# Output products, queries and expert search of a tile placed among the attention units of the next tile

## The chip, the cores and the metric
The kernel runs on one core of one Trainium2 chip. The metric is the device time of one launch in microseconds, the median over runs.

## The reference
One layer of a decoder trunk on 512 tokens of width 1024 with 16 meta tokens in front, all in float32. What is computed:

```python
xn = rms_norm(h, mix_norm_gain)
proj = xn @ w_in                     # 5320 columns: q, k, v of both mixers, indexer, two gates
a_out = diff_attention(...)          # 4 heads, two softmaxes each, causal
y_a = rms_norm(a_out, a_subln_gain) * 0.8 @ w_branch_a
b_out = dsa_attention(...)           # 8 heads over the 128 keys that the indexer picks per query
y_b = b_out @ w_branch_b
h = h + (sigmoid(gate_a) * y_a + sigmoid(gate_b) * y_b) @ w_out
hn = rms_norm(h, ffn_norm_gain)
# product-key experts, per token: 8 heads, 2 x 128 sub-keys, 16 of 128 x 128 experts a head
q = hn @ w_query; s = q . sub_keys
s1, i1 = top_k(s[0], 16); s2, i2 = top_k(s[1], 16)
top_s, top_c = top_k(s1[:, None] + s2[None, :], 16); g = softmax(top_s)
h = h + sum(g * gelu(u[expert] . hn) * v[expert])
```
u and v have 16384 rows of 1024.

## The kernel before, in words
Tokens stand in four tiles of 128. PE, DVE (VectorE), ACT (ScalarE), POOL (GpSimd) and SP (which issues the DMAs) each run a list of instructions in program order and wait on semaphores. Three blocks follow each other:

1. `project` (to about 270 us): the input projection with its weights split into high and low parts.
2. `attend`. First the attention: 48 units (`ALL_UNITS`), per tile four of kind a (one head, two softmaxes) and eight of kind b. PE's loop makes the scores of unit k, the values of unit k - 3, the transposes (`turn`) of unit k - 2 and, beside a units, two indexer scores of the next tile (L796 to L836). DVE takes the maxima (`max_of`, L1029), combines the two softmaxes of an a unit (`combine`), and searches the 128 best indexer scores of a tile in 16 rounds (`rounds`, L1000): twelve in the b units of the tile before, four in the tile's own a units (`LATE_ROUNDS`), then `mask` makes the bias that the b scores of this tile wait for (`bias_ready`). ACT does the exponents and copies the transposes (`pT`). `read_a` and `read_b` take the values out of banks 6 and 7. After all units come the outputs, tile by tile: `turn_outs`, `branch` (L873, weights w_b and w_a), `mix` (gates), `turn_mixed` (L882), `output` (L892, w_out), `residual`. w_b, w_out and w_a lie whole in SBUF: 8 MB in three DMAs.
3. `route`. Queries of four tiles (`query`: L1297 transposes, L1307 product with wq, 4 MB loaded at the block's start; `turn_query`), then the columns of u: for n = 0 to 127 a column of 128 experts is multiplied with the tokens of three tiles (L1347 to L1349, 24 products a column), with ACT splitting off the high part of u (`u_high`), POOL the low part (`u_low`, L1500), ACT the gelu, SP the store into `act_mat`. Between them: the routing product `score(i)` of a tile (L1332), DVE's search `chosen(i)` for it, and the gates of tile i as products of one-hot rows (`one_hot` on DVE, L1635; `gates` on PE, L1374, 32 groups beside 16 columns). Tile 0 goes another way: its 128 experts a token are fetched row by row by POOL's indirect DMAs (`gather`, L1509) and multiplied by DVE (`dot`, L1575), in a ring of six. `dot_plan` writes out beside which column each dot stands; `GATHER_AT` says in front of which `u_low` POOL issues each gather, and a gather waits until the dot six before it is done. `AHEAD`, `STARTS`, `TURNS_AT` place the columns: 30 ahead of tile 1's gates, 18 ahead of those of tiles 2 and 3, 14 in the tail.

`experts` (L1793 on PE) then multiplies the stored activations and gates with v, from about 1368 us to the end; POOL gathers tile 0's v rows and DVE adds them up (L1851).

The order in DVE's list after attention is this:
```python
chosen(0)
for i in range(1, NT):
    chosen(i)
    one_hot(i)
```

## Time and profile before
| | us |
|---|---|
| median of three runs (1902.97 to 1916.68) | 1914.89 |
| the profiled execution | 1911.93 |
| its span, first to last instruction | 1910.2 |
| PE busy in it | 1791.6 |
| DVE busy | 1351.9 |
| ACT busy | 715.2 |
| POOL busy | 667.8 |

The span is what the profile shows; the execution's own time lies 1.7 us above it. "Busy" of PE counts pipelined matmuls, one row may stand for several overlapping ones; a 128x512 float32 product gives two records. "PEclk" is the granted clock of TensorE as a share of 2.4 GHz.

### The profile page before, as it was taken

The numbers are of one execution on the slowest core, as the hardware profiler recorded it, in microseconds if no ns is written. First come the engines' busy times: TensorE is split into PE (matmuls) and PEld (weight loads), VectorE is DVE, ScalarE is ACT, GpSimd is POOL, SyncE is SP. The second block draws the span as 40 slices with busy tenths as digits, with TensorE's granted clock in tenths as the row PEclk, the third lists the DMA queues.
The fourth block names the chain that finished last, engine by engine and source line by source line (L and its number), as shares of the span: only waits on it lengthen the run. The fifth ranks groups of instructions, "written<-read, shape, count | busy, mean of one in ns | idle before, by whom it ended". The sixth has DMA issues, their size and how long they took to land.

```text
span 1910.2 us, 24774 instructions
## 1 busy us (share of the span) xinstructions
PE 1791.6 (94%) x8767; PEld 1492.7 (78%) x8767; DVE 1351.9 (71%) x2674; ACT 715.2 (37%) x1192; POOL 667.8 (35%) x416
## 2 busy tenths in 40 slices
PE   5899997998898899999989998999899999999998
PEld 4788875666443469999989998999788888888886
DVE  6843337783321139999978997996598888888886
ACT  4333333343110124355425543554243434343432
POOL 3224320000000105757675667678622222222220
PEclk9899996798899989999989998999999999999999
DMA  3122211001000305768887888889999999999993
GB/s 124 67 79 98 89 73 82 1 1 45 1 0 20 134 26 157 234 193 282 281 315 251 283 280 314 267 280 336 381 400 335 329 330 333 338 330 330 328 345 116
DMA packets 147359, 392.02 MB, mean 205 GB/s; under 512 B 14640, under 2 KB 65456, under 8 KB 142528
## 3 DMA queue, kind: packets, MB, share of 16 engines
q1 hardware_dynamic: 110224, 256.48, 39.2%
q0 software_dynamic: 36864, 134.23, 19.3%
q8 instruction: 55, 0.90, 0.2%
q14 instruction: 40, 0.33, 0.1%
q10 hardware_dynamic: 176, 0.07, 0.0%
HBM read 346.69 MB, written 44.04 MB: 205 GB/s over the span
## 4 chain that ended last, share of the span: by engine, by line
PE 58%; DMA 4%; POOL 3%; DVE 2%; issue 1%; ACT 0%; DVEq 0%; SPq 0%; ACTq 0%; POOLq 0%
PE psum L1793 27%; PE psum L1347 7%; PE psum L1348 7%; PE psum L1349 7%; PE psum L1374 4%; PE psum L1307 3%; POOL ul L1500 2%; PE psum L1332 1%; DMA qT<-in_u_rows,gu 1%; DMA act_mat<-act_w 1%; POOL qT L1509 1%; DMA u<-in_u 1%; DMA gate<-gate_mat 1%; DMA rows_sb<-in_u_rows,gu 1%; DVE hot L1635 0%
## 5 line engine op out<-in xcount | busy, mean ns | idle before, releaser
L1500 POOL TENSOR_TENSOR ul<-u,uh 128x1024 fp32r<-128x1024 f32 x128 | 325.9, 2549 | 543.4 <-ACT uh L1411 542.3
L1347 PE MATMUL psum<-xh_r,uh 128*128 128x384 f32 x1024 | 355.3, 347 | 19.3 <-POOL ul L1500 19.3
L1348 PE MATMUL psum<-xl_r,uh 128*128 128x384 f32 x1024 | 345.5, 337 | 0.0
L1349 PE MATMUL psum<-xh_r,ul 128*128 128x384 f32 x1024 | 345.3, 337 | 0.0
L1773 POOL DMA_INDIRECT v_row<-in_v,gv x128 | 123.7, 967 | 377.9 <-DVE psum L1851 366.9
L1347 PEld LDWEIGHTS psum<-xh_r,uh 128*128 128x128 f32 x1024 | 195.0, 190 | 23.4 <-POOL ul L1500 22.9
L1348 PEld LDWEIGHTS psum<-xl_r,uh 128*128 128x128 f32 x1024 | 195.0, 190 | 0.0
L1349 PEld LDWEIGHTS psum<-xh_r,ul 128*128 128x128 f32 x1024 | 194.5, 190 | 0.0
L1793 PE MATMUL psum<-vl,wh_rest 128*128 128x512 f32 x576 | 178.6, 391 | 0.0
L1851 DVE SCALAR_TENSOR_TENSOR psum<-v_row,w,psum 128x1024 f32<-128x1024 f32 x127 | 162.7, 1281 | 0.0
L1411 ACT CAST uh<-u 128x1024 fp32r<-128x1024 f32 x128 | 133.7, 1044 | 62.1 <-DMA u<-in_u 61.9
L1418 ACT ACTIVATE act_w<-psum 128x384 f32<-128x384 f32 x128 | 62.9, 492 | 245.0 <-PE psum L1349 238.0
L1820 ACT COPY gate<-stage 128x128 f32 (+1 forms) x126 | 37.6, 299 | 296.6 <-PE psum L1793 280.8
L322 POOL TENSOR_TENSOR wlo<-wraw,whi 128x2048 fp32r<-128x2048 f32 (+1 forms) x20 | 87.4, 4369 | 167.9 <-ACT whi L486 167.9
L613 PE MATMUL psum<-whi,xTh 128*128 128x512 f32 (+1 forms) x344 | 135.7, 394 | 9.4 <-DVE rot L395 4.7
L614 PE MATMUL psum<-wlo,xTh 128*128 128x512 f32 (+1 forms) x344 | 134.5, 391 | 0.0
L615 PE MATMUL psum<-whi,xTl 128*128 128x512 f32 (+1 forms) x344 | 133.3, 387 | 0.0
L1793 PEld LDWEIGHTS psum<-vl,wh_rest 128*128 128x128 f32 x576 | 108.2, 188 | 24.0
L1456 ACT COPY stage<-psum 128x512 f32<-128x512 f32 x96 | 104.7, 1104 | 57.3 <-PE psum L1374 57.3
L1635 DVE TENSOR_TENSOR hot<-iota,psum 128x1024 f32<-128x1024 f32 x96 | 116.8, 1217 | 12.8 <-PE psum L1362 12.1
L1793 PE MATMUL psum<-vh_first,wl 128*128 128x512 f32 x384 | 121.2, 397 | 0.0
L1793 PE MATMUL psum<-vh_second,wh_rest 128*128 128x512 f32 x384 | 118.5, 390 | 2.4 <-DVE wl L1838 2.4
(282 smaller groups left out, 3442.3 us busy)
## 6 DMA issues: line engine op xcount, KB each, us to landing
u<-in_u SPq DMA_DIRECT2D x128, 512.0 KB, 4.9
v<-in_v SPq DMA_DIRECT2D x64, 1024.0 KB, 5.0
act_mat<-act_w SPq DMA_DIRECT2D x128, 192.0 KB, 4.9
act_v<-act_mat SPq DMA_DIRECT2D x64, 384.0 KB, 7.0
wraw<-in_w_wide SPq DMA_DIRECT2D x18, 1024.0 KB, 5.2
gate_mat<-stage SPq DMA_DIRECT2D x16, 1024.0 KB, 6.4
gate<-gate_mat SPq DMA_DIRECT2D x128, 128.0 KB, 6.0
w_out<-in_w_out SPq DMA_DIRECT2D x1, 4096.0 KB, 17.3
```

Of the source, the lines that this page charges most:

```text
L613: nc.tensor.matmul(ps, xh, wh, start=(part == 0 and k == 0), stop=False)
L614: nc.tensor.matmul(ps, xh, wl, start=False, stop=False)
L615: last = nc.tensor.matmul(ps, xl, wh, start=False, stop=(part == PIECES - 1 and k == PK - 1))
L1347: nc.tensor.matmul(out, high[:, c], xh[:, c], start=(c == 0), stop=False)
L1348: nc.tensor.matmul(out, high[:, c], xl[:, c], start=False, stop=False)
L1349: last = nc.tensor.matmul(out, low[:, c], xh[:, c], start=False, stop=(c == DC - 1))
L1411: nc.scalar.copy(uh[:, n % UH_COLS], u[:, n % U_COLS]).then_inc(s["u_high"], 1)
L1500: nc.gpsimd.tensor_tensor(ul[:, n % U_COLS], u[:, n % U_COLS], uh[:, n % UH_COLS].bitcast(F32), ALU.subtract).then_inc(s["u_low"], 1)
L1635: nc.vector.tensor_tensor(hot[:, b], keys, bcast(turned[:, 0:2, some], 3, N_KEYS), ALU.is_equal).then_inc(s["hot_rows"], 1)
L1773: nc.gpsimd.indirect_dma_start(out=rows_sb[k % V_RING][:], out_offset=None, in_=d.v.rearrange("j i n -> (j i) n"), in_offset=bass.Indirect ...
L1793: mm = nc.tensor.matmul(bank(m, 2 * i + half), lhs, rhs[:, half * 512:(half + 1) * 512], start=first and k == 0 and p == 0, stop=last and ...
L1851: nc.vector.scalar_tensor_tensor(mixed0, rows_sb[n % V_RING][:], m.w0[:, n:n + 1], mixed0, ALU.mult, ALU.add).then_inc(s["mixed"], 1)
```

## The change
`attend` and `route` become one block, `mix_and_route`, on one scale of steps: step k is unit k of attention for k < 48, and steps 48 to 62 follow it. `phase_of(step, t)` counts from the start of tile t + 1, and at each phase one part of tile t's output side stands at the end of the step:

```diff
+TURN_OUTS, BRANCH_B, BRANCH_A, TURN_MIXED, OUT_LEFT, OUT_RIGHT = 3, 4, 5, 6, 7, 8
+SQUARES, ROOTS, TURN_HN, QUERY_LEFT, QUERY_RIGHT, TURN_Q = 9, 10, 11, 12, 13, 14
+LAST_STEP = NT * UNITS + TURN_Q
+FIRST_COLUMN = NT * UNITS + TURN_OUTS
+W_PIECES = 12
+W_SLOTS = 4
+GATHERED = NT - 1
+ROUTE = [0, 1, GATHERED, 2]
+SCORE_FIRST, SCORE_FIRST_REST, SCORE_SECOND = 33, 34, NT * UNITS + 2
+FIND_AT = ((40, 41, 42, 43, 44), (52, 53, 54, 55, 56))
+PAIR_AT = (45, 57)
+BEST_AT = (46, 58)
+PICK_AT = ((48, 49, 50, 51), (59, 60, 61, 62))
+SETTLE_AT = (52, 63)
+TAIL_COLUMNS = LAST_STEP - FIRST_COLUMN + 1
+    def phase_of(step, t):
+        return step - UNITS * (t + 1)
```
PE's list:
```diff
+            for step in range(LAST_STEP + 1):
+                if step < len(ALL_UNITS):
+                    for key in scores_of_unit(*ALL_UNITS[step]):
+                        score_of(*key)
+                if 2 <= step < len(ALL_UNITS) + 2:
+                    turn(*ALL_UNITS[step - 2])
+                if 3 <= step < len(ALL_UNITS) + 3:
+                    value(*ALL_UNITS[step - 3])
+                if (NT - 1) * UNITS + 2 <= step < NT * UNITS + 2:
+                    turn_last_meta(*ALL_UNITS[step - 2][1:])
+                if step < len(ALL_UNITS):
+                    for key in scores_beside(*ALL_UNITS[step]):
+                        score_of(*key)
+                beside(step)
...
+                if step >= FIRST_COLUMN:
+                    column(step - FIRST_COLUMN)
+            pe.wait_ge(s["s_out"], 4)
+            route(2, 0, 2)
+            route(2, 1, SIDE)
+            alone(FIRST_PAIR, FIRST_PAIR + 4)
+            pe.wait_ge(s["s_out"], 6)
+            route(3, 0, 2)
+            route(3, 1, SIDE)
+            alone(FIRST_PAIR + 4, TURNS_AT[1])
```
and in `beside(step)` of PE, for every tile t with j = phase_of(step, t):
```diff
+                    if j == TURN_OUTS:
+                        turn_outs(t)
+                    elif j == BRANCH_B:
+                        branch(t, 0)
+                    elif j == BRANCH_A:
+                        branch(t, 1)
+                    elif j == TURN_MIXED:
+                        pe.wait_ge(s["mixed_ready"], t + 1)
+                        turn_row(s["mixed_turned"])
+                    elif j in (OUT_LEFT, OUT_RIGHT):
+                        pe.wait_ge(s["mixedT_ready"], t + 1)
+                        half = int(j == OUT_RIGHT)
+                        half_product(W_PIECES * t + 4 + 2 * half, mixedT, half)
+                    elif j == TURN_HN:
...
+                        pe.wait_ge(s["hn_ready"], t + 1)
+                        turn_row(s["hn_turned"])
+                    elif j in (QUERY_LEFT, QUERY_RIGHT):
+                        pe.wait_ge(s["hnT_ready"], t + 1)
...
+                    elif j == TURN_Q:
+                        pe.wait_ge(s["q_out"], 2 * t + 2)
+                        turn_row(s["q_turned"])
```
DVE's list; its own `beside` follows PE's by one phase (gates after each branch, the sum, the residual, root, hn, hnT and its split), and `sub_squares(t)` and `sub_norm(t)` stand in steps 12 t + 8 and 12 t + 11:
```diff
+            for step in range(LAST_STEP + 2):
+                i, kind, h = ALL_UNITS[step] if step < len(ALL_UNITS) else (NT, "a", step - len(ALL_UNITS))
+                if kind == "a" and h == 3 and i >= 1:
+                    read_b(i - 1)
+                if kind == "b" and h == 3:
+                    read_a(i)
+                if i < NT:
+                    for key in scores_of_unit(i, kind, h):
+                        max_of(*key)
+                beside(step)
+                if i < NT and kind == "a":
+                    if i == 0:
+                        rounds(0, ROUNDS // A_HEADS * h, ROUNDS // A_HEADS)
...
+                    combine(i, h)
+                    if h == (A_HEADS - 1 if i == 0 else 0):
+                        mask(i)
+                if kind == "b" and i + 1 < NT:
...
+                    rounds(i + 1, ROUNDS * h // B_HEADS, ROUNDS // B_HEADS)
+                chosen_beside(step)
...
+            chosen(2)
+            one_hot(1)
+            chosen(3, 2)
+            one_hot(2)
+            for k in DOTS_AT[("gap", 3, 0)]:
+                dot(k)
+            one_hot(3)
```
`chosen_beside` does the search of tiles 0 and 1 in the pieces listed above (`find` in five passes over 16 rows, `pair_up`, `best`, four `pick_out`, `settle`). The other edits:

- The a and b values share one PSUM bank (`VALUE_BANK`, 5), the transposes have bank 4, and everything beside has banks 6 and 7 (`SIDE`). `value(i, "b", 0)` waits for `a_read`, `value(i, "a", 0)` for `b_read`.
- The four weight matrices come in pieces of 1 MB (512 columns of four row blocks), twelve a tile, loaded again for every tile, into four slots:

```diff
+            def load_piece(p):
+                t, j = divmod(p, W_PIECES)
+                if p >= W_SLOTS:
+                    sp.wait_ge(s["pieced"], p - W_SLOTS + 1)
...
+                sp.dma_start(w_ring[p % W_SLOTS], w[:, 4 * chunk:4 * chunk + 4, half * 512:(half + 1) * 512]
+                             ).then_inc(w_loaded[p % W_SLOTS], 16)
```
- Twelve u columns stand in steps 51 to 62. The first four loads of u are issued at step 40, the first three `u_high` at step 49.
- Tile 3 (`GATHERED`), in place of tile 0, is gathered; the columns take tiles 0 to 2. Searches are done in the order of `ROUTE`: tiles 0, 1, 3, 2. The outputs are stored in the order 3, 0, 1, 2.
- The dots move: eight stay in the search before tile 2's gates, the eight before tile 3's gates become 28 (`GAP_DOTS`), spread over its 18 columns, and 8 instead of 28 are left for the tail. The first six gathers stand at column 31 instead of 18:

```diff
-FIRST_GATHERS = 18
+FIRST_GATHERS = 2 * TURNS_AT[1] + 1
-        if i >= 2:
+        if i == 2:
             plan += [("chosen", i, j, 2 * STARTS[i] + 10) for j in range(CHOSEN_DOTS)]
+        if i == 3:
+            plan += [("gap", i, j, 2 * STARTS[i] + j * 2 * AHEAD[i] // GAP_DOTS) for j in range(GAP_DOTS)]
```
- ACT takes the square roots of a tile (`ROOTS`) in phase 10, between exponents.
- Queries of a and b lie together (`abqT`), and many buffers of SBUF get other places; nothing else of `project` and `experts` changes.

## Rows read from the trace of the kernel before
**Rows 1.** The page's busy times of all engines.
```profile
PE 1791.6 (94%) x8767; PEld 1492.7 (78%) x8767; DVE 1351.9 (71%) x2674; ACT 715.2 (37%) x1192; POOL 667.8 (35%) x416
```
**Rows 2.** Stages: length; busy us (instructions) of PE, PEld, DVE, ACT, POOL; PEclk, DMA share, GB/s.
```profile
327.00:484.00 157.00, 141.60 (x685) 99.46 (x684) 102.98 (x241) 63.24 (x189) 0.00 (x0) 0.84 0.04 14
484.00:703.00 219.00, 191.66 (x547) 94.70 (x546) 50.81 (x78) 24.54 (x37) 6.99 (x3) 0.94 0.09 34
703.00:839.00 136.00, 134.60 (x785) 133.51 (x786) 129.12 (x463) 54.65 (x71) 80.97 (x35) 0.98 0.58 178
...
1119.00:1205.00 86.00, 77.83 (x440) 77.48 (x439) 69.33 (x229) 29.74 (x41) 58.25 (x26) 0.94 0.83 298
1300.00:1364.00 64.00, 61.31 (x344) 58.44 (x342) 31.71 (x54) 21.33 (x30) 50.95 (x36) 1.00 0.98 358
```
**Rows 3.** PE in order of time: start us, us, instruction, [idle before <- releaser].
```profile
442.10 1.19 PE L796 MATMUL psum<-bkT,bqT 128*128 128x512 f32 x1 [4.69 <-DVE bias L1023]
...
489.61 1.09 PE L861 MATMUL psum<-ident,out_b 128*128 128x128 f32 x4 [5.36 <-DVE out_a L1098]
...
625.49 1.19 PE L1307 MATMUL psum<-wq,hnT 128*128 128x512 f32 x1 [5.15 <-DMA wq<-in_w_query]
```
**Rows 4.** PE, transposes of successive b units in tiles 1, 2 and 3.
```profile
353.77 0.90 PE L822 MATMUL psum<-ident,probs 128*128 128x128 f32 x3
...
357.09 0.90 PE L822 MATMUL psum<-ident,probs 128*128 128x128 f32 x3
...
405.96 0.66 PE L822 MATMUL psum<-ident,probs 128*128 128x128 f32 x4
...
408.50 0.66 PE L822 MATMUL psum<-ident,probs 128*128 128x128 f32 x4
...
459.35 0.77 PE L822 MATMUL psum<-ident,probs 128*128 128x128 f32 x5
...
462.57 0.66 PE L822 MATMUL psum<-ident,probs 128*128 128x128 f32 x4
```
**Rows 5.** PE, a branch product and eight transposes.
```profile
546.68 7.03 PE L873 MATMUL psum<-w_a,outT 128*128 128x512 f32 x16
...
597.50 1.04 PE L882 MATMUL psum<-ident,mixed 128*128 128x128 f32 x8
```
**Rows 6.** PE, start of column 12, routing product after column 27, gap before tile 3's gates.
```profile
758.63 0.44 PE L1347 MATMUL psum<-xh_r,uh 128*128 128x384 f32 x1
...
827.10 3.50 PE L1332 MATMUL psum<-keysT,qT 64*128 64x128 f32 x32
...
1177.59 0.69 PE L1347 MATMUL psum<-xh_r,uh 128*128 128x384 f32 x1 [8.17 <-POOL ul L1500]
```
**Rows 7.** DVE, starts of search passes, pairing, picks, settling; then the next tile's search.
```profile
704.98 3.19 DVE L1554 MAX8 val<-s_sb 128x8 f32<-128x128 f32 x16 [24.02 <-ACT s_sb L1442]
...
724.35 1.74 DVE L1583 CAST idx_f<-idx 128x256 f32<-128x256 uint32 x1
...
738.95 1.82 DVE L1597 TENSOR_TENSOR hits<-top_at_f,iota 128x1600 f32<-128x1600 f32 x1
...
766.29 0.82 DVE L1603 CAST pick_i<-pick 128x128 int32<-128x128 f32 x1
...
771.37 0.49 DVE L1554 MAX8 val<-s_sb 128x8 f32<-128x128 f32 x2
```
**Rows 8.** DVE groups: busy us, mean ns | idle before, releasers.
```profile
L1106 DVE TENSOR_TENSOR gates<-gates,psum 128x1024 f32<-128x1024 f32 x4 | 4.9, 1222 | 22.9 <-PE psum L873 22.9
...
L1000 DVE MAX8 maxima<-score 128x8 f32<-128x528 f32 x16 | 11.3, 704 | 0.2
```
**Rows 9.** ACT, a table load and what follows it.
```profile
820.33 1.28 ACT L1446 ACT_TABLE_LOAD   x1
821.63 0.31 ACT L1446 ACTIVATE top<-top 128x128 f32<-128x128 f32 x1
```
**Rows 10.** The page's DMA issues: count, KB each, us from issue to landing.
```profile
wraw<-in_w_wide SPq DMA_DIRECT2D x18, 1024.0 KB, 5.2
```

More of the change, by code:

```diff
@@ L85 @@
 STEP_BANKS = (0, 1, 4, 5, 6, 7)
-KB = 1024
 BASE = 16896
+TOP = 228288
+ROW = 4 * D
 def rows_of(i):
@@ new lines, in branch @@
+            def branch(t, k):
+                for half in range(2):
+                    if k == 0:
+                        pe.wait_ge(s["outT_ready"], 2 * t + half + 1)
+                    else:
+                        pe.wait_ge(s["branch_read"], 4 * t + half + 1)
+                    w = piece(W_PIECES * t + 2 * k + half)
+                    for c in range(4):
+                        last = nc.tensor.matmul(bank(m, SIDE + half), headT[:, 4 * k + c], w[:, c],
+                                                start=(c == 0), stop=(c == 3))
+                    last.then_inc(s["pieced"], 1)
@@ new lines, in turn_row, with half_product @@
+            def turn_row(sem):
+                for c in range(DC):
+                    last = nc.tensor.transpose(bank(m, SIDE, 2)[:, c * P:(c + 1) * P], row[:, c * P:(c + 1) * P], m.ident[:])
+                last.then_inc(sem, 1)
+            def half_product(p, src, half):
+                for chunk in range(2):
+                    w = piece(p + chunk)
+                    for c in range(4):
+                        last = nc.tensor.matmul(bank(m, SIDE + half), src[:, 4 * chunk + c], w[:, c],
+                                                start=(chunk == 0 and c == 0), stop=(chunk == 1 and c == 3))
+                    last.then_inc(s["pieced"], 1)
@@ L1548, in search @@
[L1548 to L1558 removed]
+            link = chain(dve, s["dve_order"])
@@ L1587, in chosen, with best @@
                 link(pairs(code, idx_f[:]))
-                link(search(top, top_at, cand, PEER_HEADS))
+            def best():
+                for part in range(5):
+                    link(search(part, top, top_at, cand, PEER_HEADS))
                 link(nc.vector.tensor_copy(top_at_f[:], top_at[:]))
```

1239 lines of the change are left out of this document (581 added, 658 removed).

## The prediction
> **What bounds the kernel now.** I read the page first: PE is busy for 94% of the span, DVE for 71%, and no other engine for half of it [rows 1]. So I asked for the stages [rows 2]. From 327 us (the first scores of attention tile 1) to 839 us (the first one-hot gates) three stages follow: the rest of attention, the output products and queries (484 to 703), and the first 30 columns of u. PE is idle in them for 15.4, 27.3 and 1.4 us; where it idles, DVE is late with the bias of a tile, the output side starts from nothing, or a stage's weights are only then loaded [rows 3]. The mean clocks 0.84, 0.94 and 0.98 say that PE ran for 50, 26 and 5 us at 1.2 instead of 2.4 GHz. An attention step of tile 1 took 3.32 us at the low level, one of tile 2, with more keys, 2.54 us at the high one [rows 4]. From 703 us on PE is full but for two gaps in front of the later tiles' gates and a tail paced by something else. So this is a kernel bound by PE: work that is moved beside other PE work saves nothing by itself. What can be saved is PE's waits and its slow clock.
>
> **PE's work from 327 to 839 us, at the high clock.** Attention: a b unit takes 2.54 us in tile 2 and 3.22 us in tile 3 [rows 4], and I put tile 1's at 1.95 us (one block less again); with the a units this makes 30 + 41 + 42 us, and 6 us to drain, 119 us. Outputs and queries: a branch product of one tile is 6.9 us for 16 matmul records, so the output product (32 records) and the query product (32) take 14 us each; eight transposes 1.04 us [rows 5]. A tile has 2 branches, output, queries and four such turns: 14 + 14 + 14 + 4 = 46 us, four tiles 184 us. (A record group of 16 took 7.03 us with its overlap, 6.9 from start to start.) One routing product 3.5 us, three lie in this stretch; a column (827.10 - 758.63 - 1.4 of wait) / 16 = 4.19 us, 30 of them 126 us [rows 6]. Sum 439 us of 512 us, so 73 us are waits (44) and slow clock (29).
>
> **What the change does to this stretch.** The same products are issued; the fourth routing product comes in front of the first gates: 443 us of work. The sum rests on how much of the 73 us of waits remains.
> Gone: the bias wait (the mask is made at a0, with all searching rounds in the b units before it), the 5.4 us before the first output transposes, the 5.2 us for the query weights [rows 3], the two block starts.
> New: in every tile a chain PE-ACT-DVE of a dozen links now sits in PE's own queue among the units. PE waits in order: while it waits for `mixed_ready`, `mixedT_ready`, `hn_ready`, `hnT_ready`, or for `a_read` (a and b values share one bank now), the scores, turns and values of the next unit stand behind it, and DVE's next maximum behind these. One 1024-wide operation of DVE takes 1.22 us [rows 8]; so much cost the sum, hnT and the low split, and a branch gated in two halves 1.4 us. Between them DVE does two rounds per b unit, each a search of the maxima at 0.70 us for 528 keys [rows 8] and a replacement that I take as long: 3 us.
> Tile 1: after branch A, DVE needs a maximum, gate and sum, 3.1 us, from a score that PE gives at 0.8; PE has 1.9 us of own work: 2 us of wait. Then rounds and read_a against turn and score: 1 us, mixedT 1.3 us. In b5 to b7 PE has 2 us a step and DVE 3.3 to 3.9: 3.3 us at `hn_ready`. With 1 us at outT 9 us. Tile 2, by the same count: 12.5 us, hnT of tile 0 (2.5 us) among it.
> Tile 3 is the worst, since DVE now also does tile 0's expert search there: five passes of 3.2 to 4.3 us (19.4 together), 14.6 us for pairing and best candidates, 27.3 us for the four picks, 5 us to settle: 66 us [rows 7]. Clocked from the end of branch A: the mix is summed at 4.6 (PE ready 3.2), turned 5.7; the search pass lets read_a end at 9.7, mixedT at 12.3 (PE ready 9.1 after its wait): PE's b2 and b3 end at 19.3 instead of 14.5. b4 to b6: PE 16.6 us, to 36; DVE ends the pairing at 37.6 and `best` at 46.6, hn at 49; PE arrives at 39.2 and waits 9.8 us. In sum 15 us, and 5 us in the units ahead: 20.
> Steps 48 to 62: 116 us of PE work (queries of tile 2, all of tile 3, 12 columns) against some 102 us of DVE work (two sets of picks 55, five passes 19, pairing and best 15, the chain's own 13). The columns fill the links; left are 3.7 us at `hn_ready` behind `best`, and 3.9 us at hnT behind a pick.
> Waits: 9 + 12.5 + 20 + 7.6 = 49 us.
> Slow clock: no row shows this mixture. Dense products beside the units should hold the clock high, and after gaps of 7 to 8 us the clock was low for a while: the stage 1119 to 1205 has a mean of 0.94, 10 us low, 5 us lost, behind its 8.17 us gap [rows 2, 6]. I take three such losses, 15 us. From below nothing at all is lost; from above the 29 us of before and once more as much.
> So the first gates come at 327 + 443 + 49 + 15 = 834 us, 5 us sooner. The 12 columns in the chain are no gain of their own: they are PE work that is done 12 x 4.2 us earlier, and cover for it.
>
> **Beside it.** Weights: 12 MB a tile in 1 MB pieces, 48 MB instead of 12. A piece is used for 3.5 us, and the nearest load of this size landed in 5.2 us [rows 10]; four slots are refilled as each is released, and every piece has at least one other product ahead of it, so I take zero; uncovered it is 1.7 us a piece, 82 us. The table switches: root and exponent now alternate within a tile's attention, two more table loads a tile at 1.28 us each [rows 9], under DVE's rounds or search in that step, zero; if not covered 2.6 us a tile. The next activation starts 0.02 us behind the load. The Trainium skill, "ScalarE: Activation LUTs", section "What ACT_TABLE_LOAD costs", puts 1.38 us of draining on top of the 1.28 us, 2.66 us in all; by it, uncovered, it would be 5.3 us a tile and the whole 21 instead of 10 us. No row here shows that drain.
> Second stretch of columns (935 to 1024 us): its routing product is gone, -3.5 us; tile 2's search with eight dots stays, and the gap by POOL with it. Third stretch: no search, 28 dots evenly. The 8.17 us gap came as POOL's gathers stood in front of `u_low` and waited for dots behind DVE's search [rows 6]; without it 18 columns take 75.4 us, plus 2 us because POOL issues 1.6 gathers a column. Before, that window took 86 us for 440 matmul records, which at 24 a column are these 18 columns [rows 2]: -8 us. Tail: 344 matmul records in 64 us [rows 2] are 14.3 columns at 4.47 us each, with two gathers a column on POOL; now 8 gathers in 14 columns, so PE's 4.19: -4 us. The start of the v stage, whose first values wait for DVE and ACT, -2 us (0 to -6). The u gathers start only 31 columns in: six take POOL some 7.5 us while DVE turns its first gates: +2 us (0 to +5). The v stage itself: 0.
>
> **Sum.** -5 - 3.5 - 8 - 4 - 2 + 2 = -20.5. The profiled execution took 1911.9 us (span 1910.2), 3 us below the median of the three runs, 1914.9. 1911.9 - 20.5 = **1891 us**, 1.2% below the median. A difference of 1% is about what a measurement of this kernel can tell from none.
>
> **Rivals.**
> 1. The waits nearly vanish: DVE is ahead of PE in most steps (it has 103 us of work in 157 us of attention [rows 2]), dense products keep the clock high. For it: DVE's sums per tile lie under PE's except in tile 3. Against: links of one step follow each other within that step. Of the 64 us some 35 go: 1856 us.
> 2. It ends slower: DVE's search and PE's products take turns instead of overlapping. Each product waits for DVE's gate, each gate for the product; a search pass that gets between is added to both. Passes, pairing and picks of two tiles are 2 x 61 us [rows 7]; in my count 24 us of them stand in PE's way. It decides once more than 46 us do; if half do, 61 us, the time is 1891 + 37 = 1928 us. For it: 703 to 839 us shows DVE busy 129 of 136 us with two of these searches, so there is no air in it. Against: there PE ran through beside them.
> 3. The weights come late: +82 us, 1973 us. For it: four times the bytes; against: the DMA share is 0.04 in attention [rows 2].
> 4. It does only what it says in the tail (the gathers), while attention and outputs take as long as before: -16 us, 1896 us.
>
> **Chances.** Forecast 0.52, rival 1 0.22, rival 2 0.12, rival 3 0.02, rival 4 0.12. The range 1848 to 1925 us takes in rival 1 and most of rival 2's ground; it leaves out some 0.1 on either side. Faster by over 1% (below 1895.7): rival 1, and 0.38 of the forecast and rival 4: 0.60. Slower by over 1% (above 1934): half of rival 2, rival 3 and some unforeseen: 0.10. Within 1%: 0.30.
>
> **What would show it.** Right: the first one-hot gates at 825 to 845 us; the longest PE wait of tile 3 at the transposes of hn in step 47, 8 to 11 us, named DVE; waits at mixed and mixedT of 1 to 3 us; clock low for some 30 us in place of 81; third gap gone, second still there with 7 us; tail columns at 4.2 us. Wrong: PE waiting for w_ring's DMAs; the clock at 1.2 GHz through whole tiles; gates(1) waiting for gathers by more than 5 us; or a first gate before 810 or after 860 us.

## The result and the profile after

The changed kernel took 1895.0 us (median of 7 runs, 1893.4 to 1897.4) against 1913.0 us (7 runs, 1901.8 to 1916.7) of the kernel before beside it: ratio 0.992, 95% interval 0.9894 to 0.9945. I had forecast 1891 us, 20.5 us less than the profiled execution of before; the profiled executions are 18.6 us apart in span (1910.2 and 1891.6 us). The gain, 0.9% by the medians and 0.8% by the ratio, stays just inside 1%; I had given 0.60 to a gain of more than that.

The page's busy times after, to hold against [rows 1]: PE has lost 13 us of busy time and keeps its 94%.

```profile
PE 1778.4 (94%) x8763; PEld 1481.9 (78%) x8767; DVE 1344.3 (71%) x2705; ACT 721.4 (38%) x1206; POOL 663.1 (35%) x416
```

The stages after, in the columns of [rows 2]: first scores of tile 1 to the first gates; then second stretch of columns, gates of tile 1 behind it, third stretch, gates of tile 2, tail:

```profile
324.00:829.00 505.00, 464.21 (x2045) 325.96 (x2050) 330.39 (x1028) 151.32 (x315) 86.19 (x35) 0.94 0.42 138
...
924.00:1010.10 86.10, 79.96 (x457) 79.29 (x455) 73.67 (x235) 31.94 (x42) 60.12 (x26) 0.96 0.84 303
1010.10:1102.50 92.40, 92.40 (x620) 91.99 (x621) 91.14 (x123) 54.33 (x61) 65.19 (x45) 1.00 0.86 280
1102.50:1190.80 88.30, 82.06 (x458) 79.57 (x457) 33.30 (x55) 27.50 (x37) 66.84 (x45) 0.98 1.01 399
1190.80:1283.10 92.30, 92.30 (x622) 91.96 (x622) 91.02 (x123) 56.10 (x64) 67.69 (x46) 1.00 0.89 295
1283.10:1350.00 66.90, 59.37 (x346) 59.08 (x345) 9.09 (x16) 22.74 (x34) 37.93 (x22) 0.97 0.73 242
```

and the same cuts of the kernel before, from the last group of one-hot products of one set of gates to the first of the next (the last ends at the first value product):

```profile
327.00:839.00 512.00, 467.86 (x2014) 327.66 (x2014) 282.91 (x782) 142.42 (x296) 87.97 (x38) 0.92 0.20 66
934.00:1026.00 92.00, 84.79 (x488) 83.83 (x486) 71.74 (x235) 33.52 (x44) 57.56 (x26) 0.94 0.79 283
1118.40:1207.30 88.90, 80.73 (x458) 80.14 (x456) 71.87 (x236) 31.49 (x42) 59.46 (x26) 0.94 0.82 293
1299.70:1368.20 68.50, 61.65 (x347) 58.80 (x345) 33.68 (x56) 23.69 (x34) 54.80 (x39) 0.99 0.98 359
```

| stage, by PE's instructions | before | after | difference | forecast |
|---|---|---|---|---|
| start to the first hot product | 841.5 | 831.5 | -10.0 | -5 |
| second stretch of columns | 92.0 | 86.1 | -5.9 | -3.5 |
| third stretch | 88.9 | 88.2 | -0.6 | -8 |
| tail and start of the v stage | 68.4 | 66.8 | -1.6 | -4 and -2 |
| three sets of gates | 277.3 | 277.2 | -0.1 | +2 |
| v stage | 534.6 | 534.2 | -0.3 | 0 |

4.0 of the first 10.0 us lie ahead of everything that was changed: attention's first scores start at 275.8 instead of 279.9 us. In the traces of the experiments, which have the same projection, they start anywhere from 275.8 to 279.5 us. So the change is worth 6.0 us there, and 14.6 us in all by these two traces.

Where PE waits now, in order of time (instruction, [idle before <- releaser]):

```profile
301.34 0.82 PE L965 MATMUL psum<-bkT,abqT 128*128 128x144 f32 x2 [5.90 <-DVE bias L1412]
...
508.33 1.13 PE L1057 MATMUL psum<-w_low,headT 128*128 128x512 f32 x2 [2.52 <-DVE headT L1502]
...
582.06 2.93 PE L1057 MATMUL psum<-w_low,mixedT 128*128 128x512 f32 x3 [1.92 <-ACT mixedT L1244]
...
617.77 1.54 PE L1050 MATMUL psum<-ident,row 128*128 128x128 f32 x6 [6.05 <-DVE row L1498]
...
709.15 1.09 PE L1050 MATMUL psum<-ident,row 128*128 128x128 f32 x8 [2.18 <-DVE row L1498]
718.04 1.22 PE L1057 MATMUL psum<-w_low,headT 128*128 128x512 f32 x1 [3.61 <-DVE headT L1502]
...
980.97 0.69 PE L1115 MATMUL psum<-split,uh 128*128 128x384 f32 x1 [6.02 <-POOL ul L1359]
...
1126.35 0.45 PE L1115 MATMUL psum<-split,uh 128*128 128x384 f32 x1 [1.96 <-POOL ul L1359]
...
1155.48 0.44 PE L1115 MATMUL psum<-split,uh 128*128 128x384 f32 x1 [2.32 <-POOL ul L1359]
...
1349.92 1.19 PE L1825 MATMUL psum<-vh_first,wh 128*128 128x512 f32 x2 [7.53 <-DVE wl L1870]
```

The three of [rows 3] are gone, and no matmul waits for a weight piece. The longest wait of tile 3's attention is the one forecast, at the norm `hn` of tile 2. In the third stretch the one gap of 8.17 us [rows 6] has turned into five, 6.2 us together.

The reason for the third stretch stands on ACT (group; busy, mean ns | idle before, releasers) and in the transfers of that window (GB/s in 40 slices, then the sum):

```profile
L1275 ACT CAST uh<-u 128x1024 fp32r<-128x1024 f32 x18 | 18.9, 1050 | 48.4 <-DMA u<-in_u 48.4
L1282 ACT ACTIVATE act_w<-psum 128x384 f32<-128x384 f32 x18 | 8.8, 490 | 13.2 <-PE psum L1117 6.5 <-DMA act_mat<-act_w 5.5 <-issue 1.0
```
```profile
GB/s 167 348 357 180 314 409 418 415 426 420 418 419 413 426 408 415 401 423 420 415 418 423 412 423 412 416 421 426 414 416 412 426 426 415 416 418 417 414 420 414
DMA packets 10087, 35.26 MB, mean 399 GB/s; under 512 B 1111, under 2 KB 3360, under 8 KB 9058
```

Before rounding u columns ACT waits for their loads, 48 us in sum; after its first slices the transfers run flat at some 416 GB/s, and the stretch has a mean of 399 GB/s and a DMA share of 1.01. The 20 extra gathers of 0.52 MB have filled the path that the columns' own loads need, as three runs below show. By the Trainium skill, "DMA: Bandwidth & Descriptors", section "Where 436 GB/s comes from", the ceiling of the path into the buffers is 435 GB/s, and for transfers between memory and buffers the memory's side binds, near 358 GB/s a core. The trace's 416 GB/s stay 4% below the first, which agrees; the second did not hold here, with one core at work, and the measurement decides.

### The profile page after: what moved, and what is told of

Its sections match the earlier page's. It is cut to its first block, busy times and chain, and to the rows that moved or that the text cites. A ratio compares the mean times of both kernels' runs of the same rounds, so it can differ in the third digit from the quotient of the medians.

```text
span 1891.6 us, 24841 instructions
## 1 busy us (share of the span) xinstructions
PE 1778.4 (94%) x8763; PEld 1481.9 (78%) x8767; DVE 1344.3 (71%) x2705; ACT 721.4 (38%) x1206; POOL 663.1 (35%) x416
## 4 chain that ended last, share of the span: by engine, by line
PE 70%; DVE 9%; DMA 3%; ACT 1%; issue 1%; POOL 1%; DVEq 0%; ACTq 0%
PE psum L1825 28%; PE psum L1115 8%; PE psum L1116 7%; PE psum L1117 7%; PE psum L1057 6%; PE psum L1141 5%; PE psum L1044 3%; PE psum L965 3%; DMA u<-in_u 2%; PE psum L1013 1%; DVE hits L1576 1%; DVE hits L1573 1%; DVE score L1390 1%; DVE pick L1577 1%; DMA act_mat<-act_w 1%
## 5 line engine op out<-in xcount | busy, mean ns | idle before, releaser
L1115 PE MATMUL psum<-split,uh 128*128 128x384 f32 x1024 | 355.7, 347 | 12.3 <-POOL ul L1359 12.2
L1117 PE MATMUL psum<-split,ul 128*128 128x384 f32 x1024 | 344.0, 336 | 0.0
L1116 PE MATMUL psum<-split,uh 128*128 128x384 f32 x1024 | 343.8, 336 | 0.0
L1825 PE MATMUL psum<-vl,wh 128*128 128x512 f32 x768 | 240.8, 395 | 0.0
L1115 PEld LDWEIGHTS psum<-split,uh 128*128 128x128 f32 x1024 | 193.8, 189 | 16.7 <-POOL ul L1359 15.0
L1116 PEld LDWEIGHTS psum<-split,uh 128*128 128x128 f32 x1024 | 193.6, 189 | 1.4 <-issue 1.4
L1117 PEld LDWEIGHTS psum<-split,ul 128*128 128x128 f32 x1024 | 193.1, 189 | 0.0
L1825 PEld LDWEIGHTS psum<-vl,wh 128*128 128x128 f32 x768 | 144.8, 189 | 33.9
L621 PE MATMUL psum<-whi,xTh 128*128 128x512 f32 (+1 forms) x344 | 135.1, 393 | 10.6 <-DVE rot L404 5.7
L1865 DVE TENSOR_TENSOR gate<-gate,act_v 128x384 f32<-128x384 f32 x128 | 73.6, 575 | 87.5 <-DMA act_v<-act_mat 46.2
L1544 DVE SCALAR_TENSOR_TENSOR rows_sb<-rows_sb,psum 128x1024 f32<-128x1024 f32 x86 | 104.0, 1217 | 35.5 <-DMA rows_sb<-in_u_rows,tri 35.5
L1825 PE MATMUL psum<-vh_first,wh 128*128 128x512 f32 x384 | 121.8, 398 | 7.5 <-DVE wl L1870 7.5
```

Of the source, the lines that this page charges most:

```text
L621: nc.tensor.matmul(ps, xh, wh, start=(part == 0 and k == 0), stop=False)
L1115: nc.tensor.matmul(out, high[:, c], split[:, 0:DENSE, 0, c], start=(c == 0), stop=False)
L1116: nc.tensor.matmul(out, high[:, c], split[:, 0:DENSE, 1, c], start=False, stop=False)
L1117: last = nc.tensor.matmul(out, low[:, c], split[:, 0:DENSE, 0, c], start=False, stop=(c == DC - 1))
L1825: mm = nc.tensor.matmul(bank(m, 2 * i + half), lhs, rhs[:, half * 512:(half + 1) * 512], start=first and k == 0 and p == 0, stop=last and ...
```

## The experiments

All start from the changed kernel. Of each, the median stands with the ratio to runs of the kernel before taken beside it (95% interval), then the stage lengths of its one trace, cut as above. "Start to gates" is from the first scores to the first hot product, so that the start of attention drops out.

| kernel | median us | ratio | start to gates | second | third | tail | v stage |
|---|---|---|---|---|---|---|---|
| before | 1913.0 | | 561.7 | 92.0 | 88.9 | 68.4 | 534.6 |
| changed | 1895.0 | 0.992 (0.9894 to 0.9945) | 555.7 | 86.1 | 88.2 | 66.8 | 534.2 |
| 8 dots in third | 1891.5 | 0.987 (0.9825 to 0.9919) | 556.0 | 88.6 | 78.3 | 69.6 | 538.8 |
| 18 dots in third | 1884.4 | 0.984 (0.9792 to 0.9885) | 555.8 | 87.6 | 80.9 | 66.4 | 533.9 |
| small stores | 1893.7 | 0.989 (0.985 to 0.9937) | 555.5 | 95.9 | 80.1 | 66.1 | 533.8 |
| search early | 1882.3 | 0.984 (0.9791 to 0.988) | 541.4 | 88.8 | 88.7 | 66.2 | 533.2 |
| v gathers late | 1894.8 | 0.990 (0.9864 to 0.993) | 555.5 | 87.6 | 87.6 | 62.0 | 538.3 |
| columns last | 1919.4 | 1.003 (1.0009 to 1.0046) | 578.9 | 86.1 | 88.1 | 66.5 | 533.0 |
| two slots | 1891.6 | 0.990 (0.985 to 0.9941) | 547.7 | 86.5 | 87.6 | 65.9 | 533.6 |
| no roots | 1892.1 | 0.989 (0.9849 to 0.9926) | 551.1 | 87.7 | 88.0 | 66.5 | 533.8 |
| all | 1870.1 | 0.980 (0.9758 to 0.9838) | 541.4 | 83.2 | 79.5 | 64.7 | 535.8 |
| all but v | 1869.5 | 0.979 (0.9747 to 0.9827) | 541.4 | 82.7 | 78.9 | 65.9 | 534.3 |
| four chosen | 1865.8 | 0.974 (0.9724 to 0.9752) | 541.5 | 78.8 | 82.1 | 66.3 | 532.7 |
| none chosen | 1873.7 | 0.978 (0.9766 to 0.9797) | 541.3 | 78.3 | 84.3 | 67.6 | 536.9 |

**The third stretch: three runs.** First the dots go back to the tail, in two sizes:

```diff
-GAP_DOTS = 28
+GAP_DOTS = 8
```

> Base: the changed kernel, with only 8 dots (and 8 gathers) in the third stretch of columns instead of 28; the other 20 go back into the tail, which has 28 again. Theory A (the third stretch is bound by DMA bandwidth: 28 gathers of 0.5 MB, 18 u loads of 0.5 MB, stores of 3.4 and 8 MB are 34.4 MB, and the trace shows 416 GB/s from end to end, so 83 us for 75.4 us of columns): with 20 gathers less it is 24.4 MB, 59 us, so PE's waits for u_low there (6.2 us together) go, the stretch from the last hot product of tile 1 to the first of tile 2 falls from 88.2 to 81 us; the tail goes back to 4.47 to 4.8 us a column, +4 to +8 us. Sum -3 to +1 us: 1892 to 1896 us. Rival B (POOL's own pace: 1.6 gathers a column at 1.25 us beside 2.4 us of u_low are 4.4 us a column): the stretch falls too, to 81 to 82 us, so this run alone doesn't tell A from B. Rival C (the dots make DVE late): as B.

```diff
-GAP_DOTS = 28
+GAP_DOTS = 18
```

> Base: the changed kernel, with 18 dots in the third stretch instead of 28, so 18 in the tail of 14 columns. Theory A (bandwidth): 29.4 MB at 416 GB/s are 71 us, under the 75.4 us of the columns: nearly all of the 6.2 us of waits go, stretch 81 to 83 us; DMA share under 1. The tail stays within 1 us of its time, since POOL has 2.4 + 1.3 x 1.25 = 4.0 us a column, under 4.19: in all -5 us, 1890 us. Rival B (POOL): one gather a column is 3.65 us, under 4.19: the same stretch. Rival D (it is latency of the first loads, not the sum): the waits stay at 4 to 6 us and the time at 1895.

Then all 28 stay, and other traffic is taken out of the stretch:

```diff
-                sp.dma_start(d.gate_mat[i - 1, :, part * w:(part + 1) * w],
-                             stage[:, part * w:(part + 1) * w, :]).then_inc(s["stage_stored"], 16)
+                e = w if i == 1 else 1
+                for a in ((0, 1) if i == 1 else (1,)):
+                    sp.dma_start(d.gate_mat[a, :, part * w:part * w + e],
+                                 stage[:, part * w:part * w + e, :]).then_inc(s["stage_stored"], 16)
```

> Base: the changed kernel with all 28 gathers and dots in the third stretch, but the gates of tile 2 are not stored there: each of the 8 stores takes one key's columns instead of 16 (0.06 MB instead of 1 MB); so that the matrix is full, tile 1's gates are stored in its place as well, in the second stretch. It leaves out tile 2's gates from the output. Theory A (bandwidth): 26.9 MB in the third stretch, 65 us at 416 GB/s: PE's waits for u_low there fall from 6.2 to under 1.5 us, and the stretch from 88.2 to 82 us; ACT's waits for u in it go. The second stretch gets 8 MB more (18 columns, 8 gathers: 32 MB in 86 us) and may lose 0 to 2 us. Rivals B (POOL's pace) and C (DVE's dots): POOL and DVE do the same as before, so the waits stay at 5 to 7 us and the stretch at 87 to 89 us. Time: A 1889 to 1891, B and C 1895.

The third stretch in the three traces, in the order of the runs (one window each; columns as in [rows 2]):

```profile
1106.10:1184.40 78.30, 78.30 (x456) 78.01 (x455) 8.51 (x15) 29.87 (x39) 50.27 (x26) 1.00 0.94 333
```
```profile
1104.10:1185.00 80.90, 78.93 (x457) 77.92 (x455) 20.78 (x35) 28.48 (x38) 58.46 (x36) 1.00 0.98 376
```
```profile
1114.30:1194.40 80.10, 79.38 (x458) 78.14 (x457) 33.48 (x55) 27.15 (x36) 67.14 (x45) 1.00 0.98 344
```

In the third POOL and DVE are as busy as in the changed kernel (67 and 33 us), yet PE's waits fall from 6.2 to 0.7 us and the stretch by 8.1 us. So it was the transfers, and neither POOL's pace nor the dots. PE's waits go with the DMA share: none at 0.94, 2.0 and 0.7 us at 0.98, 6.2 us at 1.01. ACT's wait for u loads does not tell it: it is 48 us in the changed kernel, but still 36 us with 18 dots and with the small stores, and 19 us with 8, where PE waits for nothing. In bytes my theory was rough, for the narrow stores kept the share at 0.98 with only 344 GB/s. A cost I had put at 0 to 2 us came out at 9.7: with 16 MB of stores the second stretch took 95.9 us, one of its waits being 14.4 us. That is why this kernel's median is only 1.3 us lower. With 18 dots left for the tail it is as short as with 8 (66.4 against 66.8 us), as worked out; with 28 it gives back 2.8 us, and the v stage another 4.6. Eighteen is worth 10.6 us of median. The traces are 6.4 us apart: 7.3 us less in this stretch, 1.5 us more in the second.

**DVE's search against the norm.** The passes, pairing and best candidates of tiles 0 and 1 go into steps in which DVE stood idle. The largest such place, in DVE's order of time:

```profile
593.44 0.71 DVE L1418 TENSOR_REDUCE nmax<-psum 128x1 f32<-128x528 f32 x1 [12.39 <-PE psum L967]
```

```diff
-FIND_AT = ((40, 41, 42, 43, 44), (52, 53, 54, 55, 56))
-PAIR_AT = (45, 57)
-BEST_AT = (46, 58)
-PICK_AT = ((48, 49, 50, 51), (59, 60, 61, 62))
+FIND_AT = ((40, 41, 42, 43, 43), (52, 53, 54, 55, 55))
+PAIR_AT = (43, 55)
+BEST_AT = (44, 56)
+PICK_AT = ((48, 49, 50, 51), (60, 61, 62, 63))
```

> Base: the changed kernel; DVE's expert search of tiles 0 and 1 is packed forward by two steps into places where the trace shows DVE idle (12.4 us in the step of tile 2's output product, 6.8 and 6.2 us in tile 3's): passes at steps 40 to 43 with the last two in one, pairing in 43, best candidates in 44 instead of 46 (and 52 to 55, 55, 56 instead of 58); the second tile's picks start one step later, behind hnT. Same work. Theory E (PE's 6.05 us wait for the norm of tile 2, and the 2.18 and 3.61 us in tile 3, are DVE behind its own search, no more): the three go, -8 to -11 us with some clock back, 1885 to 1888 us; first hot product at 820 to 824 instead of 831.5. Rival F (DVE's total work in these steps is what binds; order does not matter): the waits only turn up elsewhere (at mixed, at the a values, in front of the first gates), sum of PE's waits from 560 to 830 us stays within 3 us: 1893 to 1897 us.

The norm's transposes in this trace, and the window from tile 2's first branch product to the first hot product in it and in the changed kernel:

```profile
614.53 0.66 PE L1050 MATMUL psum<-ident,row 128*128 128x128 f32 x4 [0.91 <-DVE row L1498]
```
```profile
551.90:819.40 267.50, 259.83 (x1263) 202.87 (x1266) 203.88 (x734) 85.36 (x131) 89.83 (x37) 0.98 0.50 161
```
```profile
550.70:831.50 280.80, 262.98 (x1263) 205.56 (x1266) 206.97 (x736) 86.44 (x131) 88.08 (x37) 0.96 0.48 154
```

The same 1263 matmul records need 13.3 us less: PE's idle time falls from 17.8 to 7.7 us, and its busy time by 3.2 us at a higher mean clock. 6.05 us have become 0.91, the 2.18 and 3.61 us are gone. DVE's total work did not bind; its order did. The median is 12.7 us below the changed kernel's, and 2.7 us of the trace's gain are lost again in the second stretch.

**The columns as cover.**

```diff
-FIRST_COLUMN = NT * UNITS + TURN_OUTS
+FIRST_COLUMN = LAST_STEP - 1
```

> Base: the changed kernel with the columns undone as cover: only the last 2 of the 12 u columns run between the steps of tile 3's outputs and queries, the other 10 behind them. Same work. Theory J (the columns fill the links of the chain PE-ACT-DVE): in steps 51 to 60 DVE has 55 us of passes, pairing, best and picks besides its links, PE loses 42 us of columns there: PE's waits from 640 to 740 us grow from about 9 us to 30 to 40 us, with low clock in them; DVE however is then no later in front of the first gates. 1918 to 1932 us. Rival K (they are cover for very little, since DVE's 12 us of chain are short): waits grow by 5 to 12 us: 1900 to 1908 us. Rival L (no cover needed): 1895 us.

Two of its PE waits, and its stretch from 640 to 740 us; then that of the changed kernel:

```profile
700.64 1.97 PE L1050 MATMUL psum<-ident,row 128*128 128x128 f32 x8 [12.61 <-DVE row L1498]
707.34 1.22 PE L1057 MATMUL psum<-w_low,headT 128*128 128x512 f32 x1 [4.74 <-DVE headT L1502]
```
```profile
640.00:740.00 100.00, 76.48 (x288) 46.48 (x287) 78.34 (x279) 18.19 (x24) 11.17 (x4) 0.86 0.36 119
```
```profile
640.00:740.00 100.00, 94.04 (x413) 69.23 (x412) 78.90 (x260) 28.43 (x37) 28.03 (x11) 0.98 0.51 167
```

DVE works as long in both (78 of 100 us). Where ten columns, 42 us of PE's work, are taken out from between the links, PE idles for 23.5 instead of 6.0 us of these 100, less than the 30 to 40 us of theory J, and at a mean clock of 0.86; the time lies in J's range. The stage is 23.2 us longer, the median 24.4 us: more than the whole change had won. With this cover gone nothing is left of the change's gain (1.003).

**Weight slots, square roots.**

```diff
-W_SLOTS = 4
+W_SLOTS = 2
```

> Base: the changed kernel with two buffers for the 1 MB pieces of the weights instead of four. Theory M (streaming costs nothing as a piece lands in about 5 us and four are ahead): with two, a piece is asked for as the one two before it is read, and each step's second piece has only the 3 to 4 us of units and the 3.5 us of its neighbour ahead of it: the waits for pieces stay under 1 us each, 0 to 10 us in all: 1895 to 1905 us. Rival N (the streaming has little margin): 1.7 us for most of 48 pieces plus low clock: +40 to +80 us.

No matmul waited for a piece with two slots either, so theory M held in its mechanism. The median was 3.4 us lower, below M's range, with runs from 1887 to 1898 us, and in the trace, which is of the fastest of them, the stage was 8 us shorter. Its waits at the norm are those of the changed kernel (6.05 and 2.18 us). Half of the 8 us lies ahead of tile 2's first branch product, the rest behind it. Chance from trace to trace is a poor explanation: five traces with the changed kernel's code up to the first gates (changed, 8 dots, 18 dots, small stores, v gathers late) took 555.5 to 556.0 us. The cause stays open.

```diff
-                        nc.scalar.activation(root[:, t:t + 1], ms[:, t:t + 1], ACT.Sqrt).then_inc(s["root_ready"], 1)
+                        nc.scalar.activation(root[:, t:t + 1], ms[:, t:t + 1], ACT.Copy).then_inc(s["root_ready"], 1)
```
(and the same for `sub_root`)

> Base: the changed kernel with the two square roots per tile on ACT replaced by copies (the norms of the sub-heads and of the stream are then not those of the reference), so that no activation table is switched between exponents and roots within a tile. Theory O (each load is 1.28 us, under DVE's work of the same step, and there is no drain behind it): the time stays within 2 us of 1895. Rival P (two more switches a tile cost 2.66 us each on the path, as the page on activation tables has it, and the chain at the norm waits for them): -5 to -20 us, 1875 to 1890 us, and the 6.05 us wait at the norm of tile 2 shrinks.

ACT at tile 1's root in the changed kernel:

```profile
489.37 1.28 ACT L1251 ACT_TABLE_LOAD   x1
490.66 0.20 ACT L1251 ACTIVATE root_r<-ms_r 128x1 f32<-128x1 f32 x1
```

Ten of the 16 loads between 275 and 840 us are gone without roots. PE's wait behind the copy of the expert scores falls from 3.06 to 1.64 us; the norm's wait stays (6.32 us). The stage is 4.6 us shorter than in the changed kernel, where five traces of the same code agree within 0.5 us, and the median 2.9 us lower; all four runs (1890.8 to 1893.0 us) lie below the changed kernel's seven. So the loads cost some 3 to 5 us, a little more than theory O allowed, and not the 21 us that two switches a tile at 2.66 us would come to on the path.

**The start of the value stage.** In the changed kernel ACT's last activation waits 6.25 us for a store. The chain of waits up to the first value product, and the issues on SP ahead of it:

```profile
1334.10 0.50 ACT act_w L1282
1334.62 13.39 DMA act_mat<-act_w
1348.17 0.32 issue
1348.49 0.30 ACT dots L1352
1348.79 0.41 ACT wh L1856
1349.22 0.57 DVE wl L1870
```
```profile
1331.05 0.39 SPq L1753 DMA_DIRECT2D v<-in_v  x1
...
1333.75 0.67 SPq L1760 DMA_DIRECT2D act_v<-act_mat  x1
1334.62 0.36 SPq L905 DMA_DIRECT2D act_mat<-act_w  x1
```

```diff
+        pool.wait_ge(s["hidden"], N_KEYS)
         for k in range(PICKS):
-            if k == V_RING - 2:
-                pool.wait_ge(s["hidden"], N_KEYS)
```

> Base: the changed kernel; the first six gathers for tile 3's value rows wait for the last column too, as the seventh does (in the changed kernel they start at 1334 us, in the kernel before at 1361.5 of 1368 us, as the dots then ended late). Theory G (PE's 7.5 us of idle time in front of the value products comes from the store of column 125's activations, issued at 1334.6 us behind 2.4 MB of early loads and beside six gathers of 0.5 MB: it landed 13.4 us later, and ACT's last activation waited for it): without the gathers it lands in some 7 us, the wait falls to 2 to 3 us, -5 us: 1890 us. The first value rows are then late for DVE's mix by 2 to 4 us, which PE does not wait for at once. Rival H (the loads ahead in the queue alone hold it): the store still takes over 11 us and the wait stays 6 to 8 us; 1895 us. Rival I: the late rows hold DVE and with it the low parts of the second product, and the wait comes back as one behind the first product: 1894 to 1897 us.

Rival I held. PE's wait fell to 2.7 us and the tail by 4.8, and the v stage took 4.1 us more: DVE stood 3.13 us for the first gathered row, ahead of the low parts of the second product. The store now landed within 8.6 us of its issue instead of 13.4, so the gathers have a share. What the loads ahead of it do is asked in the last run.

**Together.** Four edits: search early, 18 dots, two gathers of value rows ahead (`k == 2` in place of `k == V_RING - 2`), and the second stretch's gathers one to a column, against eight in a row on POOL (from 966.6 to 977.7 us, ahead of the 6.02 us wait; the three `u_low` behind them also took 3.7 us each beside DVE's picks):

```diff
-            plan += [("chosen", i, j, 2 * STARTS[i] + 10) for j in range(CHOSEN_DOTS)]
+            plan += [("chosen", i, j, 2 * STARTS[i] + 8 + j) for j in range(CHOSEN_DOTS)]
```

> Base: the changed kernel with four edits together: the search packed forward (as in e4), 18 dots in the third stretch (as in e2), only two gathers of value rows ahead of the last column instead of six or none, and the eight gathers of the second stretch spread one to a column (in the changed kernel they stand one behind the other on POOL for 11 us, 966.6 to 977.7 us, ahead of u_low, and PE waits 6.0 us at 981). Theory: each place gives what its own run gave, since they lie one behind the other on PE: first hot product -10 to -13 us, second stretch -6 (no wait left, 81 us long), third -7, the start of the value products -3 to -4 with no new wait in it (e5 won 4 us in front of them and lost 4 behind, as DVE's first mix waited for a row). Sum -26 to -30: 1865 to 1869 us. Rival Q (DVE is next: in the second stretch its search ends 1.5 us ahead of the second gates, so the stretch can't get shorter than some 84 us): second stretch -2 only, 1869 to 1873 us, and a wait at the turned picks.

> Base: e9 with the gathers of the value rows as in the changed kernel (six ahead of the last column). Theory G (the last store of activations lands late behind and beside them): PE's wait in front of the value products is 6 to 8 us again, and e9 is ahead of it by 3 to 4 us, all of it in the 66 us between the last hot product and the first value product. Rival: the two are equal within 1 us, with e9's gain lost behind the first value products.

The stages add up as their own runs had them, except for the second stretch, -2.9 of the 6 us hoped for, and the v gathers, whose win of 1.2 us in front is lost behind (1.5 us): the two kernels are equal. Rival Q's floor of 84 us, set by DVE's search, was not there: 83.2 and 82.7 us, and 78.8 below. In the second stretch three waits of 1.33 us stand where one of 6.02 was. The rows of POOL, then DVE, then PE there:

```profile
972.55 2.37 POOL L1367 DMA_INDIRECT rows_sb<-in_u_rows,tri  x1
974.93 3.25 POOL L1359 TENSOR_TENSOR ul<-u,uh 128x1024 fp32r<-128x1024 f32 x1
978.33 2.37 POOL L1367 DMA_INDIRECT abqT<-in_u_rows,tri  x1
```
```profile
972.06 2.03 DVE L1573 TENSOR_TENSOR hits<-top_at_f,iota 128x1600 f32<-128x1600 f32 x1
974.13 1.82 DVE L1576 TENSOR_TENSOR hits<-hits,code 128x1600 f32<-128x1600 f32 x1
975.99 1.82 DVE L1577 TENSOR_REDUCE pick<-hits 128x32 f32<-128x1600 f32 x1
```
```profile
978.24 0.44 PE L1115 MATMUL psum<-split,uh 128*128 128x384 f32 x1 [1.33 <-POOL ul L1359]
```

POOL and DVE run in lockstep, 5.78 us a column: a gather's issue takes 2.37 us instead of 0.95, a `u_low` 3.25 instead of 2.40. The gather of 972.55 us was issued while DVE's first product ran, and ended 0.83 us after that product (974.92 against 974.09). So fewer gathers belong beside the picks.

```diff
-CHOSEN_DOTS = 8
-GAP_DOTS = 18
+CHOSEN_DOTS = 4
+GAP_DOTS = 20
```

> Base: e10 (search packed forward, gathers of the second stretch one to a column, value rows as in the changed kernel), with 4 dots and gathers in the second stretch instead of 8, 20 instead of 18 in the third, 20 in the tail. Theory R (in the second stretch POOL and DVE slow each other: in e9 a gather's issue took 2.37 us instead of 0.95 and a u_low 3.25 instead of 2.40 beside DVE's picks, 5.77 us a column, and PE waited three times 1.33 us): with half the gathers beside the picks, one or none of the three waits stays, stretch 82.7 to 80 to 81.5 us; third stretch 79 to 80.5 us (30.4 MB, 73 us at 416 GB/s); tail +0 to +1.5 us. Sum -1 to -3 us: 1867 to 1869 us. Rival: the tail gives all of it back (20 gathers in 14 columns beside u_low are 4.2 us a column, at the edge): 1870 to 1872 us.

The last kernel has `CHOSEN_DOTS = 0` and `GAP_DOTS = 22`, two value gathers ahead, and

```diff
-                if n == N_KEYS - U_COLS:
+                if n == N_KEYS - U_COLS + 1:
                     late.load_early(sp)
```

> Base: e9 with no dots in the second stretch at all, 22 in the third and 22 in the tail, and the early loads of the value stage issued behind the store of column 125's activations instead of ahead of it. Theory R: no gather beside the picks in the second stretch, so it has no wait, 79 to 81 us; third 79.5 to 81.5 us (31.4 MB, 75.5 us at 416 GB/s, at its limit); tail +2 to +3 us as 22 gathers are 4.4 us a column on POOL. Theory S (what held the first value product is the order on the load queue: the store behind 2.4 MB of loads, not the gathers, since e9 and e10 are equal): the last activation comes at once, and the wait is then set by the loads themselves, which start 3.6 us later: 5.4 us falls to 2 to 4 us. Rival T (the loads are as late as the store was): the wait stays 5 to 7 us. Sum: -1 to -4 us with S, 1867 to 1870 us; 1870 to 1872 with T.

Second stretch, then third, of the kernel with four; last, ACT in the kernel with none:

```profile
911.80:990.50 78.70, 78.09 (x453) 77.53 (x451) 69.25 (x224) 31.43 (x42) 57.10 (x22) 1.00 0.84 303
1083.00:1165.10 82.10, 79.53 (x457) 77.85 (x456) 23.28 (x39) 27.86 (x37) 59.96 (x38) 1.00 1.00 384
```
```profile
1324.43 0.30 ACT L1839 COPY gate<-stage 128x128 f32<-128x128 f32 x1 [9.88 <-DMA act_v<-act_mat]
```

With four, theory R held, at 78.8 us even better than forecast (4 us less than with eight), and the third stretch took 3.1 us back with two more dots and a DMA share of 1.00. 1865.8 us is the fastest of all, 29 us below the changed kernel. With none, the second stretch wins 0.5 us more, while the third (84.3 us) and the tail lose 3.5 and the v stage 4.2; at 1873.7 us it is slower than either theory had it. (It also has two value gathers ahead and not six, so the 4.2 us are not those of the loads' order alone.) At the value stage rival T held: the activation no longer waits, the loads are as late as the store was, PE's wait is 6.6 us, and a second one of 2.4 us has appeared behind it. That start is bound by what has to be moved; no order that I tried shortened it, front and back together.

## Why the prediction was right, and where not

**First gates, forecast -5, found -6.0 (and 4.0 of an earlier start).** I had 443 us of work, 49 of waits and 15 of slow clock from 327 to 834 us. The trace has 505 us from 324 to 829, of which PE is idle for 40.8; with my 443 us of work 21 are left for the slow clock. The sum, 62 against 64 us, is right by luck: the two misses go opposite ways. The waits at `hn` in step 47 were 6.05 us instead of 9.8, and 2.18 instead of 3.7 in tile 3's; hnT 3.61 for 3.9; mixed and mixedT between 0.8 and 1.9, as forecast. The slow clock is the larger miss: at a mean of 0.94 some 60 of the 505 us ran at the low level (81 before), not 30. I took three losses behind long gaps. It also fell behind waits of 1 to 3 us, and tile 0 hands a slow clock on into tile 1 (low from 291 to 332 us).

**The columns beside the chain** I had called cover and no gain of their own. Taking ten out cost 24 us. This was right in kind, and I had not put a price to it; of all that the runs took out or moved it is the largest.

**Rival 2** (search and products take turns) was the true mechanism of the waits that remained, at 12 of the 24 us that I had counted into PE's way. It did not decide. That it was a matter of order, worth 13 us, I had not seen: I clocked the search against PE step by step and did not ask where DVE then stood idle.

**Second stretch, -3.5, found -5.9.** The routing product's 3.5 us left, and the gap by POOL was 6.0 us (7.2 before) where I had 7. The rest is a mean clock of 0.96 for 0.94.

**Third stretch, -8, found -0.6: the step that failed.** I wrote that without POOL's gap of 8.17 us "18 columns take 75.4 us, plus 2 us because POOL issues 1.6 gathers a column". I priced 20 moved gathers by the engine that issues them and not by the path that carries them. The row was there: that stage had a DMA share of 0.83 at 298 GB/s over 86 us [rows 2], and 20 gathers of 0.52 MB in the same time add some 122 GB/s, to 420. With the 28 gathers and the stores in place the rate was 399 in the mean and 416 where it lay flat, and the share 1.01. The gap did go; PE's waits of 6.2 us for late u columns took its place. With 18 dots the stretch took 80.9 us, which is the -8.

**Tail and start of the value stage, -6 together, found -1.6.** Up to its last wait the tail went from 64.1 to 59.3 us: its columns came at PE's pace, and the -4 was right. The -2 for the start was not. The dots being done early, the value gathers start at 1334 us, 16 us ahead of the first value product instead of 7 us, beside the early loads and the last store; PE's wait in front of that product is 7.5 us, where the kernel before had 4.3. I had written -2 without asking what the earlier end of the dots would trigger.

**At nothing:** the weights' streaming (no wait, even with two slots) was right. The table loads at zero are off by some 3 to 5 us. The late u gathers at the first gates, +2, cost nothing: 92.5 us before and after.

The total was met to 4 us. Third stretch and tail missed by 12 us together; the first gates and the second stretch gained 3.4 us more than forecast, the value stage and the gates 2.4, and 4.0 us come from the earlier start, which was no merit of the forecast. That the total came so close is in good part these misses cancelling.

## What to carry to other kernels

Where gathers are moved to an emptier place, count bytes as well as issues: add their rate to the row of the stage that gets them, and stop where the DMA share comes near 1. When a long chain is threaded through another engine's queue, look on the helping engine for idle time and put its background work exactly there: the same work up to two steps earlier gave 13 us. And keep independent work between the links. Without it this rewrite was no faster than the kernel it replaces.

## What was not expected of the hardware

- A DMA share of 0.98 was reached at a mean of 344 GB/s with narrow stores and at 376 with wide ones; at 399 GB/s in the mean the share was 1.01. The share, not the rate, told when columns came late.
- POOL's issue of a gather slowed from 0.95 to 2.37 us beside DVE's picks, and `u_low` from 2.40 to 3.25 us. The Trainium skill, "SBUF — State Buffer", section "Who interferes with whom", has a DVE operation with two inputs in the buffers contend with GpSimd's reads, and infers that it leaves the writing of descriptors alone. The first agrees with the slower `u_low`. For the issue of a gather the second does not hold here. A gather from the kernel with all but the v gathers, issued 0.08 us into such an operation, then one from the changed kernel, issued while DVE made a one-hot product whose other input lies in PSUM (835.52 to 836.74 us):

```profile
1315.70 1.23 DVE L1868 TENSOR_TENSOR vl<-v,vh_first 128x1024 fp32r<-128x1024 f32 x1 [0.32 <-ACT vh_first L1840]
1315.78 1.95 POOL L1806 DMA_INDIRECT v_row<-in_v,gv  x1 [0.30 <-issue]
```
```profile
836.05 0.94 POOL L1367 DMA_INDIRECT rows_sb<-in_u_rows,tri  x1 [0.30 <-issue]
```

  In the fourteen traces 287 gathers were issued 0.06 us or more after the start of a DVE operation with two inputs in the buffers that had at least 0.19 us left. All of them ended 0.80 to 0.83 us after that operation, up to 2.37 us after their own start. Nearly 1400 were issued while DVE ran an operation with an input in PSUM, and took 0.93 to 0.96 us each. Where issue and operation began within 0.05 us of each other (543 times, all at `gate` in the v stage), the gather took 0.94 us nearly always. So a two-input operation that already runs holds the gather's issue until it ends. The gather also reads its row numbers from the buffers; whether that reading waits or the writing of descriptors, no run shows.
- Square roots between exponentials: ACT's table load started 0.02 us after the instruction before it, and the next activation 0.01 us after the load's 1.28 us. The Trainium skill, "ScalarE: Activation LUTs", section "What ACT_TABLE_LOAD costs", has 1.38 us of draining on top of each switch; neither side of the load shows it here.
- Traces of the same code agree closely even where the clock falls often. From attention's first scores to tile 2's first branch product, where eleven kernels have the same code, their traces took 273.6 to 275.1 us; two slots had 270.8 and no roots 269.6 us. How the stage differs between executions of one kernel is not known, since each has one trace.
